# A decoder-layer kernel on one core: all streamed tiles moved to the weight ring's offset modulo 512 bytes, and the small-gate weights laid out in blocks of 128 columns

## What is computed

```python
xn = rmsnorm(x, mix_norm_g[l])
p = xn @ w_in[l]
(aq, ak, av, ao, ai, af, bb, bc, bx, cz, cxbc, cdt,
 sq, sk, sv, gates) = jnp.split(p, SPLIT_POINTS, axis=-1)
ya = mlstm(aq, ak, av, ao, ai + a_igate_b[l], af + a_fgate_b[l], a_norm_g[l])
yb = short_conv_mixer(bb, bc, bx, b_conv_w[l])
yc = mamba2_mixer(cz, cxbc, cdt, c_conv_w[l], c_conv_b[l], c_dt_bias[l], c_a_log[l],
                  c_d_skip[l], c_norm_g[l])
yd = stick_breaking_attention(sq, sk, sv)
ycat = jnp.stack([ya, yb, yc, yd], axis=2)
lifted = jnp.einsum('bsie,ied->bsid', ycat, w_lift[l])
g = jax.nn.sigmoid(gates.reshape(Bn, S, N_BRANCH, D_MODEL))
merged = jnp.einsum('bsid,bsid->bsd', g, lifted)
x = x + merged @ w_out[l]
x = x + conv_glu_mlp(rmsnorm(x, ffn_norm_g[l]), w_up[l], ffn_conv_w[l], ffn_conv_b[l], w_down[l])
...
return rmsnorm(x, final_norm_g)
```

## Time and profile before

| | |
|---|---|
| time, median of 3 runs | 1050.11 us (1050.05 to 1050.98) |
| span of the profiled execution | 1048.9 us |
| TensorE busy | 1031.9 us, 98% |
| VectorE busy | 593.3 us, 57% |
| ScalarE busy | 424.8 us, 41% |
| chain that ended last, by engine | PE 93%, DVE 4%, ACT 2% |
| transfers | 108.24 MB, mean 103 GB/s |

### The profile page before, as it was taken

One profiled execution on the slowest core, in us unless ns is written; L12 is line 12 of the kernel. 1 busy time (PEld: TensorE's weight loads), 2 busy tenths in 40 slices (PEclk: granted clock), 3 DMA queues, 4 the chain that ended last, 5 costly groups with the idle time before them and its releaser, 6 DMA issues.

```text
span 1048.9 us, 12635 instructions
## 1 busy us (share of the span) xinstructions
PE 1031.9 (98%) x4724; PEld 837.0 (80%) x4724; DVE 593.3 (57%) x764; ACT 424.8 (41%) x515; POOL 67.7 (6%) x74
## 2 busy tenths in 40 slices
PE   8999999999999999999999999989999999999996
PEld 6797888887777887777888888868888888888886
DVE  6834753766676576554454365687566566533323
ACT  5514446554435333434342334454444433423222
POOL 5610000000000000000000000400000000000002
PEclk9999999999999999999999999999999999999999
DMA  6331232223321333342242222413332232243312
GB/s 243 112 105 69 81 87 77 81 90 104 98 90 63 124 131 131 108 148 81 98 165 98 101 81 101 170 64 108 100 100 82 97 100 80 67 168 95 95 56 80
DMA packets 32024, 108.24 MB, mean 103 GB/s; under 512 B 3684, under 2 KB 5860, under 8 KB 31600
## 3 DMA queue, kind: packets, MB, share of 16 engines
q1 hardware_dynamic: 29520, 93.86, 27.1%
q0 software_dynamic: 2320, 13.69, 3.8%
q10 hardware_dynamic: 144, 0.14, 0.1%
HBM read 103.42 MB, written 4.25 MB: 103 GB/s over the span
## 4 chain that ended last, share of the span: by engine, by line
PE 93%; DVE 4%; ACT 2%; issue 1%; DMA 1%; DVEq 0%; SPq 0%; ACTq 0%
PE gb L411 81%; PE gb L444 4%; DVE w_lo L983 1%; PE xb L594 1%; PE gb L522 1%; PE xb L554 1%; PE xb L547 1%; PE xb L534 1%; PE xb L411 1%; ACT w_hi L699 1%; PE xb L511 1%; DMA raw<-w_stream 1%; DVE y_lo L991 1%; PE gb L462 1%; PE xb L582 0%
## 5 line engine op out<-in xcount | busy, mean ns | idle before, releaser
L983 DVE TENSOR_TENSOR w_lo<-raw,w_hi 128x1024 fp32r<-128x1024 f32 (+2 forms) x181 | 218.1, 1206 | 353.6 <-ACT w_hi L699 353.0
L699 ACT ACTIVATE w_hi<-raw 128x1024 fp32r<-128x1024 f32 (+2 forms) x181 | 183.8, 1017 | 424.9 <-PE gb L411 390.9
L411 PE MATMUL gb<-xn_hi,w_hi 128*128 128x512 f32 x720 | 285.7, 397 | 0.0
L411 PE MATMUL gb<-xn_lo,w_hi 128*128 128x512 f32 x720 | 282.1, 392 | 0.0
L411 PE MATMUL gb<-xn_hi,w_lo 128*128 128x512 f32 x720 | 280.7, 390 | 0.0
L411 PE MATMUL gb<-y_hi,w_hi 128*128 128x512 f32 x400 | 160.8, 402 | 5.4 <-DVE y_lo L991 3.7
L411 PEld LDWEIGHTS gb<-xn_hi,w_hi 128*128 128x128 f32 x720 | 135.6, 188 | 31.3 <-issue 1.0
L411 PE MATMUL gb<-y_hi,w_lo 128*128 128x512 f32 x400 | 159.9, 400 | 0.0
L411 PEld LDWEIGHTS gb<-xn_lo,w_hi 128*128 128x128 f32 x720 | 135.6, 188 | 29.7 <-issue 1.4
L411 PE MATMUL gb<-y_lo,w_hi 128*128 128x512 f32 x400 | 159.0, 398 | 0.0
L411 PEld LDWEIGHTS gb<-xn_hi,w_lo 128*128 128x128 f32 x720 | 135.5, 188 | 29.4
(11 more groups left out here) (231 smaller groups left out, 1018.4 us busy)
## 6 DMA issues: line engine op xcount, KB each, us to landing
raw<-w_stream SPq DMA_DIRECT2D x149, 512.0 KB, 3.3
raw<-w_down SPq DMA_DIRECT2D x16, 384.0 KB, 3.0
abc<-scr_a POOLq DMA_DIRECT2D x8, 640.0 KB, 4.2
raw<-w_down SPq DMA_DIRECT2D x16, 320.0 KB, 2.8
x_in<-xT SPq DMA_DIRECT2D x8, 256.0 KB, 6.2
x<-xT POOLq DMA_DIRECT2D x1, 2048.0 KB, 8.7
scr_x<-x POOLq DMA_DIRECT2D x1, 2048.0 KB, 7.4
x<-scr_x POOLq DMA_DIRECT2D x1, 2048.0 KB, 8.5
```

What stands on the lines that cost most here:

```text
L411: ins = pe.matmul(out, w[:, r, lo:hi], rhs(k)[x], start=(first and n == 0 and q == 0), stop=(last_ and n == len(ks) - 1 and q == 2))
L699: act.activation(w_hi[:, r, 0:n], raw[:, r, 0:n], ACT.Copy).then_inc(S["hi_ready"], 1)
L983: dve.tensor_tensor(w_lo[:, r, 0:n], raw[:, r, 0:n], w_hi[:, r, 0:n].bitcast(F32), ALU.subtract)\
```

## The change

The tile `y_hi0` is no longer placed right behind `cst` but at the next multiple of 512 bytes from the start of the map. The offset from the start was 88160 (172 x 512 + 96) and is 88576 (173 x 512), so `y_hi0` and every tile behind it move up by 416 bytes. Before, these tiles began at 224 modulo 512, `raw`, `w_hi`, `w_lo`, `xn_hi` and `xn_lo` at 128; now all of them begin at 128. (Modulo 2048 the first of them is 512 further than the ring's slots.)

The small-gate unit keeps its 96 columns for each block, but the blocks lie 128 columns (512 bytes) apart instead of 96 (384 bytes), both in the streamed array and where the matmuls read. The last 32 columns of each block are zeros and are not used.

Engines, shapes, order and waits of all instructions are as before; lines behind the new code are two higher (L411 is L413).

```diff
@@ -41,6 +41,8 @@
 PACK = sum(BLK_W)
 EPS = 1e-6
 NEG = -1e30
+
+LINE = 512
 A_HEADS, C_HEADS, D_HEADS = 4, 8, 4
 A_SCALE = 64 ** -0.5
 D_SCALE = 128 ** -0.5
@@ -165,7 +167,7 @@
     fin_g = vec[:, V_FIN:V_FIN + KD].rearrange("p (k one) -> p k one", one=1)
     rsm = m.put("rsm", [40, 4])
     cst = m.put("cst", [P, 4])
-    END_CONST = m.at
+    m.at = base + (m.at - base + LINE - 1) // LINE * LINE
     y_hi0 = m.put("y_hi0", [P, 4, T], F32R)
     y_lo0 = m.put("y_lo0", [P, 4, T], F32R)
     G0 = m.at
@@ -459,7 +461,7 @@
             elif u == U_SMALL:
                 for k in range(KD):
                     for q, (w, x) in enumerate(((w_hi, 0), (w_hi, 1), (w_lo, 0))):
-                        ins = pe.matmul(gb(o)[0:96, :], w[:, u % RING, 96 * k:96 * k + 96], xn(k)[x],
+                        ins = pe.matmul(gb(o)[0:96, :], w[:, u % RING, P * k:P * k + 96], xn(k)[x],
                                         start=(k == 0 and q == 0), stop=(k == KD - 1 and q == 2))
             else:
                 ins = gemm(gb(o)[:, :], u % RING, 0, xg if u < U_DV else xn, range(KD))
@@ -1420,9 +1422,9 @@
             stream[u + 2 * n], stream[u + 2 * n + 1] = s[:, :1024], s[:, 1024:]
 
     put(U_DQ, sq); put(U_DK, sk); put_tokens(U_DV, sv)
-    small = np.zeros((D, 96), np.float32)
+    small = np.zeros((D, P), np.float32)
     small[:, 0:4], small[:, 32:36], small[:, 64:72] = ai, af, cdt
-    stream[U_SMALL, :, 0:KD * 96] = slabs(small)
+    stream[U_SMALL] = slabs(small)
     put(U_AQ, aq); put(U_AK, ak); put_tokens(U_AV, av); put(U_AO, ao)
```

## The result

The changed kernel takes 1037.41 us (median of 4 runs, 1036.94 to 1038.42) against 1050.55 us for the kernel before on the same chips: a ratio of 0.9875, 95% interval 0.9861 to 0.9889. The forecast was 1036.3, with a range from 1034.2 to 1038.9. The profiled execution took 1038.42 us with a span of 1036.7; it is the slowest of the four.

What follows compares the result with a forecast made beforehand. TensorE's pace through its matmul queue was taken as the bound (busy 1031.9 of 1048.9 us). Terms 1.17 + 3.1 + 1.2 + 5.3 + 3.05 + 0.05 made 13.9, taken as 13.8: 1050.1 - 13.8 = 1036.3 us, range 1034.2 to 1038.9.

Steps and rivals of the forecast that it cites:

- Two speeds, bound to the tile's offset: 512-column matmuls: 226.7 ns where both reads' offsets agree modulo 512, 233.3 ns otherwise; 1036.3 us, chance 0.86.
- The forecast's own proof: Small-gate unit: aligned xn with weight blocks 384 bytes apart runs at 231.7 ns, though xn is fast everywhere else.
- Term 6: Small-gate unit: 24 matmuls from 231.7 to 226.7 ns, less those needed to settle, gain 0.05 us.
- Terms 1 to 3 and 5: Units 0 to 7 on y 1.17 us; lift units 3.1; projection and first peeled unit 1.2, loop 5.3; down-projection 3.05.
- Term 4: Other three peeled units: no gain; TensorE's 0.4 us turns into a y_lo wait of 4.1 us instead of 3.74.
- VectorE's cover: Up-projection loop: VectorE goes from 78% to 80% busy and does not become what units wait for.
- the longer half-clock stretch: Behind the y_lo wait: one half-clock stretch kept; its absence or doubling would change the time by -1.8 or +1.8 us.
- term 3: Units alternating y and xn: 0.135 us each; projection and first peeled unit 1.2 us, up-projection loop 5.3 us.
- B: Whole kernel: slow speed belongs to the tiles' place or another property, so no effect, 1050.1 us; chance 0.06.
- C: Some streams settle, others, the alternating units, don't: about half the gain, 1043 us; chance 0.04.
- D: Matmuls on y and h: period longer than 512 bytes makes them slower, +11 us, 1061 us; chance 0.04.

Runs made afterwards that it cites:

- xn_off_96: Changed kernel with xn_hi and xn_lo moved 96 bytes off the ring, y and h still on it: 1052.09 us, ratio 1.0016.
- base_96: Changed kernel with the whole map moved up by 96 bytes, so all tiles still agree with each other: 1038.12 us, ratio 0.988.
- block_only: Kernel before with only the small-gate blocks put 128 columns apart, all tiles where they were: 1050.08 us in one run.
- scan_c: Changed kernel with y_hi0/y_lo0 160 bytes off the ring, y_hi1/y_lo1 64, h 224, and full 128-column small-gate blocks: 1047.94 us in one run.
- w_lo_off: Changed kernel with only the weight ring w_lo moved 96 bytes off; w_hi, xn, y and h agree: 1056.83 us in one run.
- pad_only: Changed kernel with the small-gate blocks back at 384 bytes apart, so only the padding remains: 1037.74 us, ratio 0.9873.
- xn_off_64: Changed kernel with xn_hi and xn_lo moved 64 bytes off the ring: 1044.57 us in one run.
- scan_a: Changed kernel with y_hi0/y_lo0 256 bytes off the ring, y_hi1/y_lo1 128 and h 64: 1040.95 us in one run.
- scan_b: Changed kernel with y_hi0/y_lo0 32 bytes off the ring, y_hi1/y_lo1 384 and h 192: 1049.29 us in one run.

## Why the prediction was right, point by point

**Two speeds, bound to the tile's offset: right.** xn_off_96 and base_96 show it from both sides. The period was named too long, 256 bytes and not 512, which made no difference to a change that brings every offset to 0. The forecast's own proof was weaker than I took it for. The row of the small-gate unit was read as 5.0 ns of offset; block_only and scan_c split it into 1.7 ns of offset and 3.3 of width. I had named the width as what stood against the proof, and it was the larger part. Term 6 was 0.05 us, and the unit went from 5.58 to 5.54 us in the chain, a gain of 0.04. That agreement is luck: the term took 5.0 ns from each matmul less a large part for settling, where the runs show 24 x 1.7 ns and nothing off for settling. The line of the kernel before is

```profile
79.75 5.58 PE gb L462 x24
```

**Terms 1 to 3 and 5: right in size.** The stream from unit 2 on: 0.75 us gained between the first two lines of the table, for 118 distances of 6.6 ns 0.78. From a lift unit to the next 16.32 us as written, a unit of the loop 5.44 as written. From the long stream on xn to the loop 4.11 us, against 3.1 + 1.2 for lift units and projection. The down-projection 3.09, against 3.05. The halves of 256 columns nothing, as written.

**Term 4, the peeled units give nothing: right.** The wait for y_lo grew from 3.74 to 4.16 us, forecast 4.1, and from the sum to the first matmul behind the wait it is 24.1 us in both (668.11 to 692.23, 663.10 to 687.20).

**VectorE's cover: right.** It never became what a unit of the loop waits for after the first. From 704.33 to 905.00 it is busy 124.5 of 200.7 us, 62%; the 78% of the forecast held only for the 23 us right behind the wait. Its own instructions didn't change: xn_lo 751 ns and y_lo 753 ns, against 752 both the earlier trace rows:

```profile
L993 DVE SCALAR_TENSOR_TENSOR y_lo<-x,vec,y_hi 128x512 fp32r<-128x512 f32 x4 | 3.0, 753 | 4.3 <-ACT y_hi L893 4.3
L993 DVE SCALAR_TENSOR_TENSOR xn_lo<-x,vec,xn_hi 128x512 fp32r<-128x512 f32 x4 | 3.0, 751 | 4.1 <-ACT xn_hi L893 4.1
```

**What is missing, 13.8 forecast and 12.2 in the span.** About 1.2 us is the longer half-clock stretch, the term that I had kept at one stretch of 3.4 us. From the end of the wait to the end of the loop the kernel gained 4.09 us where term 3 gives 5.3, since matmuls went at half clock for 5.7 us, until 692.9, instead of for 3.4 us, from 692.8 to 696.2. I had bounded a double stretch by 1.8 us; the profiled execution had one, cheaper by the 1.0 us that lies in the wait. Another 0.3 us was lost at the very start, where the stream begins at 10.25 instead of 9.95 because the first weights came later (6.11 us from issue to landing in the chain instead of 5.82); that goes with the transfer and not with matmuls. By the medians the gain is 13.1 us, from 1050.55 to 1037.41; the forecast had started from 1050.11.

In the traces at hand the double stretch goes with the longer wait. Where the wait for y_lo is 3.72 to 3.81 us (before, block_only, w_lo_off, xn_off_96) the clock is at its lower level for 3.4 us; where it is 3.85 to 4.16 us (the changed kernel, pad_only, base_96, the scans, xn_off_64) for 6.8. It need not be so in every execution: two of the four runs of the changed kernel have a span of 1035.2 us, next to the 1035.1 of the forecast, but only the slowest of the four was profiled, so which stretch the others had is not shown.

**The rivals.** B (no effect) is refuted for this stream: moving one of the two reads by 96 bytes changes the distance by 6.7 ns, wherever the tile lies. The Trainium skill, "TensorE: Matmul & The Clock Gate", Part 2, says that loading the next weights takes no bandwidth from the running matmul. These runs differ in what follows from it: with only w_lo moved, 226.7 ns became 232.6, so the pace of the matmuls depends on where the weights lie that are being loaded. What the two reads have in common is not shown. C (some streams settle, others don't) didn't happen in the changed kernel, but w_lo_off shows that the condition behind it is real. D (a longer period) is refuted: the period is shorter, 256 bytes.

What stays open is the mechanism itself. The offsets that are fast, a third as costly and slow (0, 64, the rest) and the two speeds at 256 columns would have to follow from it; I have no theory that gives them.

## What to carry to other kernels

All of this was measured on fp32r matmuls with a new stationary block for each. When TensorE is busy all the time, measure the distance from start to start for each tile that it streams, not the mean duration; a few nanoseconds on thousands of matmuls are a per cent. If groups of the same shape differ, compare the offsets of stationary and moving operand modulo 256 bytes and pad small constants so that all rings and tiles agree, the weight rings among themselves too, since one that is out of step spoils the others. And where TensorE waits some microseconds for a fixed chain, a faster stream ahead of it only lengthens the wait, and in these traces the half-clock stretch around its end; matmuls without a purpose in the wait were worth 2 us here.

## What the runs showed of the hardware that I had not expected

- The offsets tried repeat after 256 bytes, and an offset of 64 is a third as costly as others: 228.9 ns against 233.3, where 0 gives 226.7.
- Narrow stationary blocks are slower to stream over: 96 columns 230.0 ns a matmul, 128 columns 226.7, in the same aligned place.
- With 256 moving columns alignment gives nothing: 120 ns in step and with the moving tile 96 bytes ahead (before, h), 117.8 with it 64 ahead (scan_a, h), 113.6 with it 192 ahead (scan_b, h), and 117.8 and 114.0 with the stationary tile 64 ahead in one and the same kernel (xn_off_64). With the stationary tile 96 ahead it is 117.3 (xn_off_96).
- One weight ring of two out of step, 96 bytes, takes the whole stream to 232.6 ns.
- Around the end of a wait of 4.16 us TensorE's granted clock was at its lower level for 6.8 us, of which the first 1.0 still lay in the wait; around a wait of 3.74 us it was so for 3.4 us. With work in the wait and 0.6 us of it left, it did not fall.
